# Last norm token-major with the store, weight splits moved to VectorE and ahead, and the router's transpositions placed among the rows'

## The reference, cut to what matters

```python
def _rmsnorm(x, g):
    return x * rsqrt(mean(x * x, axis=-1) + EPS) * g

# layer 0: Hyena channels, two orders, then the output projection
for o in range(HYENA_ORDER):
    z = gates[o] * _fftconv(z, kf[:, o], p['filt_bias'][o])
yl = concatenate([y_a, z]) @ p['w_out']

# layer 1: conformer
u = h @ p['cf_w1'] + p['cf_b1']
u = u[..., :D_MODEL] * sigmoid(u[..., D_MODEL:])
u = _dwconv_vertical(u, p['cf_dw_w'], p['cf_dw_b'], rows)
yl = silu(_layernorm(u, p['cf_ln_g'], p['cf_ln_b'])) @ p['cf_w2'] + p['cf_b2']

# both layers
xl = xl + g1 * yl
h = _modulate(_rmsnorm(xl, norm2_g[l]), sh2, sc2)
probs = softmax(einsum('bnd,de->ben', h, router), axis=experts)
gates, idx = top_k(probs, cap)          # every expert takes its 64 best tokens
xl = xl + g2 * (experts' outputs, weighted and added back)

return _rmsnorm(xl, final_g)
```

## Time and profile before

| | us |
|---|---|
| median of 3 runs | 3064.94 (3060.89 to 3071.62) |
| profiled execution, device time | 3064.76 |
| its span | 3063.0 |
| PE busy, of the span | 2473.9 (81%) |
| PEld | 1524.5 (50%) |
| DVE | 1330.0 (43%) |
| ACT | 601.3 (20%) |
| POOL | 266.8 (9%) |

### The profile page before, as it was taken

The page is one execution under the profiler, slowest core; times in us unless marked ns, Lnnn a source line. Parts: engine busy times, 40 slices in busy tenths (PEclk is TensorE's granted clock), DMA queues, the critical chain, the costliest instruction groups (busy, mean ns, idle before and its releaser), DMA issues. The chain is left out here.

```text
span 3063.0 us, 42592 instructions
## 1 busy us (share of the span) xinstructions
PE 2473.9 (81%) x18456; PEld 1524.5 (50%) x18456; DVE 1330.0 (43%) x2123; ACT 601.3 (20%) x868; POOL 266.8 (9%) x165
## 2 busy tenths in 40 slices
PE   5987499888999997359366678998986787889896
PEld 3775499764554553337223463443435564434343
DVE  4876755445232323469545641211216843112214
ACT  3333311122111111432400130110003132100011
POOL 2000000111000000120302230000003211000000
PEclk7997599988999998679658789999998888999998
DMA  4580111145999994157010329999983135999994
GB/s 150 179 281 12 35 39 39 45 166 247 418 407 418 417 418 169 55 170 243 22 47 28 112 83 416 427 428 428 428 340 83 55 139 220 427 428 428 428 427 193
DMA packets 123082, 726.90 MB, mean 237 GB/s; under 512 B 11958, under 2 KB 67510, under 8 KB 85879
## 3 DMA queue, kind: packets, MB, share of 16 engines
q1 hardware_dynamic: 92776, 695.79, 56.1%
q10 hardware_dynamic: 30160, 28.97, 2.9%
HBM read 722.63 MB, written 2.10 MB: 237 GB/s over the span
## 5 line engine op out<-in xcount | busy, mean ns | idle before, releaser
L1962 PE MATMUL ps<-s_ring,s_c_XG 128*64 128x512 f32 x1280 | 351.0, 615 | 57.5 <-DMA s_ring<-in_exp_w 25.7
L332 PE MATMUL ps<-s_h_part,s_w_hi 128*128 128x512 f32 x944 | 300.1, 400 | 77.2 <-PEq L433 62.9
L2074 DVE TENSOR_TENSOR s_c_hid<-ps,s_c_sil 128x512 f32<-128x512 f32 x32 | 34.3, 1073 | 515.2 <-PE ps L1962 515.2
L1962 PEld LDWEIGHTS ps<-s_ring,s_c_XG 128*64 128x64 f32 x1280 | 118.0, 141 | 279.2 <-issue 278.0
L1962 PE MATMUL ps<-s_ring_at,s_c_XG 128*64 128x512 f32 x768 | 238.1, 627 | 22.9 <-DMA s_ring_at<-in_exp_w 19.2
L332 PEld LDWEIGHTS ps<-s_h_part,s_w_hi 128*128 128x128 f32 x944 | 181.7, 194 | 121.9 <-issue 72.2
L2003 PE MATMUL ps<-s_ring_at,s_c_hidT 128*64 128x512 f32 x768 | 223.2, 593 | 0.0
L1962 PE MATMUL ps<-s_ring,s_m_XG 128*64 128x512 f32 x768 | 222.7, 593 | 0.0
L332 PE MATMUL ps<-s_h_part,s_w_lo 128*128 128x512 f32 x472 | 187.4, 397 | 0.0
L373 DVE CUSTOM_DVE_ANT_0 s_mod_w<-s_mod_w,s_mod_silu 128x1024 f32<-128x1024 f32 x112 | 135.1, 1221 | 42.8 <-DMA s_mod_w<-in_vectors 42.6
L1962 PEld LDWEIGHTS ps<-s_ring,s_m_XG 128*64 128x64 f32 x768 | 71.1, 137 | 142.7 <-issue 141.6
(11 more groups left out here) (584 smaller groups left out, 4434.0 us busy)
## 6 DMA issues: line engine op xcount, KB each, us to landing
s_ring<-in_exp_w SPq DMA_DIRECT2D x96, 2048.0 KB, 16.4
s_ring_at<-in_exp_w SPq DMA_DIRECT2D x96, 2048.0 KB, 18.6
s_ring<-in_moe_w_gate SPq DMA_DIRECT2D x32, 2048.0 KB, 12.2
s_ring_at<-in_moe_w_down SPq DMA_DIRECT2D x32, 2048.0 KB, 12.3
s_mod_w<-in_vectors SPq DMA_DIRECT2D x112, 512.0 KB, 4.5
s_ring<-in_moe_w_up SPq DMA_DIRECT2D x16, 2048.0 KB, 12.7
s_ring_at<-in_moe_w_up SPq DMA_DIRECT2D x16, 2048.0 KB, 16.3
s_w_raw<-in_w_in ACTq DMA_DIRECT2D x21, 1024.0 KB, 7.7
```

The source lines that it names most:

```text
L332: last = nc.tensor.matmul(bank, w[a][:, i % 2, k, c0:c0 + P], x[b][:, k, at], start=start, stop=stop)
L1962: last = nc.tensor.matmul(ps[x * SLOTS:(x + 1) * SLOTS, bank + fh, :], XG[:, k, c0:c0 + SLOTS], w[x][:, at:at + 512], start=(k == 0), stop ...
L2074: nc.vector.tensor_tensor(hid_out[:, fh * per:(fh + 1) * per, :], ps[:, UP + fh, :].rearrange("s (p j) -> s p j", j=nj), sil[:, fh * 512:( ...
```

## The change

1. The last norm and the store become one block, `norm_and_store`. TensorE transposes `xT` itself; per token tile ScalarE squares both halves from PSUM and sums them along the row in the same instruction, VectorE makes the mean of squares, ScalarE the root, VectorE the reciprocal of one column and two multiplies from PSUM by it and by the gains. The gains are tiled over the partitions on the host (`final_g_2_row`, 512 KB) and loaded by SyncE behind the last refill of the last expert pass, into a fixed place.
2. In `conformer_in` the lower halves of units 2 to 7 are made by VectorE, between `u` of m and its taps. GpSimd has nothing there.
3. In `residual_route_choice` the transpositions of `wts` stand behind the fifth of the eight row groups and write to the `LOGITS` bank; the last row group, which needs that bank, waits for VectorE's copy. The subtraction of one is done by the last copy out of PSUM.
4. In `hyena_conv`, order 1, ScalarE and VectorE split units 0 and 1 of `w_out_2`, once `B` is written.

```diff
@@ tensor_tiles ends with the sums; its last loop becomes
-                for j, (n, half) in enumerate(self.rows):
+            def tensor_rows(self, pe, first, end):
+                for j in range(first, end):
+                    n, half = self.rows[j]
                     if self.ROW_BANKS[j] == self.SUMS:
                         pe.wait_ge(self.ms_done.sem, 1)
                     if self.ROW_BANKS[j] == self.LOGITS:
@@ residual_route_first
                     R.tensor_tiles(pe, 1)
+                    R.tensor_rows(pe, 0, 2 * KT)
@@ residual_route_choice
-            PROBS, RANK = R.ROW_BANKS[0], R.ROW_BANKS[1]
+            PROBS, RANK = R.LOGITS, R.ROW_BANKS[1]
...
                     R.tensor_tiles(pe, P)
-                    pe.wait_ge(R.row_out.sem, 2)
+                    R.tensor_rows(pe, 0, 5)
                     pe.wait_ge(dve_out.sem, v0 + 2)
                     for t in range(KT):
                         last = nc.tensor.transpose(ps[0:E, PROBS, t * P:(t + 1) * P], wts[:, t, :], ident)
                     last.then_inc(*mm_done.up())
+                    R.tensor_rows(pe, 5, 2 * KT - 1)
                     pe.wait_ge(dve_out.sem, v0 + 3)
+                    R.tensor_rows(pe, 2 * KT - 1, 2 * KT)
+                    pe.wait_ge(R.row_out.sem, 2)
+                    pe.wait_ge(dve_out.sem, v0 + 4)
...
-                    vlink(V.tensor_copy(work[0][:], ps[0:E, PROBS, :]))
+                    V.tensor_copy(work[0][:], ps[0:E, PROBS, :]).then_inc(*dve_out.up())
+                    dve.wait_ge(dve_out.sem, dve_out.n)
...
-                    vlink(V.tensor_tensor(rk[:], rk[:], sel[:], ALU.mult))
-                    V.tensor_scalar(rk[:], rk[:], -1.0, None, ALU.add).then_inc(*dve_out.up())
+                    V.tensor_tensor(rk[:], rk[:], sel[:], ALU.mult).then_inc(*dve_out.up())
                     dve.wait_ge(mm_done.sem, m0 + 2)
-                    V.tensor_copy(rankm[:], ps[:, RANK, 0:KT * E].rearrange("p (t e) -> p t e", t=KT))
+                    V.tensor_scalar(rankm[:], ps[:, RANK, 0:KT * E].rearrange("p (t e) -> p t e", t=KT), -1.0, None, ALU.add)
@@ experts_pass, end of SyncE's list
+                        if load_also is not None:
+                            load_also(sp)
@@ hyena_conv, ScalarE and VectorE
+                        if o == HYENA_ORDER - 1:
+                            act.wait_ge(dve_out.sem, v0 + HF)
+                            ahead.split_hi(act, 0)
+                            ahead.split_hi(act, 1)
+                            ahead.early = True
...
+                        if o == HYENA_ORDER - 1:
+                            ahead.split_lo_unit(dve, 0)
+                            ahead.split_lo_unit(dve, 1)
                         for c in range(CT):
                             dve.wait_ge(mm_done.sem, m0 + 2 * HF + c + 1)
@@ conformer_in
-                    @block.gpsimd
-                    def _(pool):
-                        W.split_lo(pool, W.next_unit())
...
+                        for i in range(W.next_unit(), 2):
+                            W.split_lo_unit(dve, i)
                         for m in range(KD):
                             dve.wait_ge(act_out.sem, a0 + m + 1)
                             nc.vector.scalar_tensor_tensor(u[:, m, :], ps[:, 2 * (m % 4), :], vcol("cf_b1_2", m), sig[:, m % 2, :], ALU.add, ALU.mult).then_inc(*dve_out.up())
+                            W.split_lo_unit(dve, m + 2)
@@ store_result becomes norm_and_store(gain, gain_here)
                         for t in range(KT):
-                            sp.wait_ge(dve_out.sem, v0 + t + 1)
-                            sp.wait_ge(act_out.sem, a0 + t + 1)
+                            sp.wait_ge(scaled_rows.sem, 2 * t + 2)
                             sp.dma_start(out[t * P:(t + 1) * P, :], rows[:, t, :]).then_inc(*stored.up(16))
...
-                                    last = nc.tensor.transpose(ps[:, 2 * t + half, c * P:(c + 1) * P], src[:, half * 4 + c, t * P:(t + 1) * P], ident)
-                                last.then_inc(*mm_done.up())
+                                    last = nc.tensor.transpose(ps[:, 2 * t + half, c * P:(c + 1) * P], xT[:, half * 4 + c, t * P:(t + 1) * P], ident)
+                                last.then_inc(turned.sem, 1)
...
                         for t in range(KT):
-                            act.wait_ge(mm_done.sem, m0 + 2 * t + 2)
-                            nc.scalar.activation(rows[:, t, 512:1024], ps[:, 2 * t + 1, :], ACT.Copy).then_inc(*act_out.up())
+                            for half in range(2):
+                                act.wait_ge(turned.sem, 2 * t + half + 1)
+                                nc.scalar.activation(square[:, half, :], ps[:, 2 * t + half, :], ACT.Square, accum_out=part[:, t, half:half + 1]).then_inc(summed.sem, 1)
+                            act.wait_ge(meaned.sem, t + 1)
+                            nc.scalar.activation(root[:, t:t + 1], ms[:, t:t + 1], ACT.Sqrt).then_inc(rooted.sem, 1)
...
+                        dve.wait_ge(gain_here.sem, 16)
                         for t in range(KT):
-                            dve.wait_ge(mm_done.sem, m0 + 2 * t + 1)
-                            nc.vector.tensor_copy(rows[:, t, 0:512], ps[:, 2 * t, :]).then_inc(*dve_out.up())
+                            at = slice(t, t + 1)
+                            dve.wait_ge(summed.sem, 2 * t + 2)
+                            vlink(V.tensor_tensor(ms[:, at], part[:, t, 0:1], part[:, t, 1:2], ALU.add))
+                            V.tensor_scalar(ms[:, at], ms[:, at], 1.0 / D, RMS_EPS, ALU.mult, ALU.add).then_inc(meaned.sem, 1)
+                            dve.wait_ge(rooted.sem, t + 1)
+                            vlink(V.reciprocal(rstd[:, at], root[:, at]))
+                            for half in range(2):
+                                to = slice(half * 512, (half + 1) * 512)
+                                V.scalar_tensor_tensor(rows[:, t, to], ps[:, 2 * t + half, :], rstd[:, at], gain[:, to], ALU.mult, ALU.mult).then_inc(scaled_rows.sem, 1)
@@ calls
+        def load_final_gain(sp):
+            at = vec_at["final_g_2_row"]
+            sp.dma_start(final_gain[:], A["vectors"][:, at:at + D]).then_inc(final_gain_here.sem, 16)
...
-            moe_choice(1, W, hT, weight(1, 1), part(1, 3), part(1, 5), part(1, 2), vcol("cf_b2_2", 0, KD))
-        with ExitStack() as last:
-            fin = sbuf(last, "fin", [P, KD, T])
-            rms_norm(xT, fin, T, lambda k: vcol("final_g_2", k))
-            store_result(fin)
+            moe_choice(1, W, hT, weight(1, 1), part(1, 3), part(1, 5), part(1, 2), vcol("cf_b2_2", 0, KD), load_final_gain)
+        norm_and_store(final_gain, final_gain_here)
```

21 lines of the change are left out of this document (16 added, 5 removed).

## The result

The changed kernel takes **3032.39 us** (median of 4 runs, 3030.24 to 3033.6), the kernel before 3063.02 in the same comparison (4 runs, 3060.89 to 3071.62). The ratio is 0.9903 with a 95% interval of 0.9889 to 0.9917: 30.6 us faster, by the interval 25 to 34. The forecast was 3036, its range 3028 to 3046.

A forecast was written before the change was run, and what follows sets the result against it. DMA engines were taken to bound both expert passes of the second model, so gains came from chains ahead and outside. 8.2 + 3.5 + 4.5 + 13.0 = 29.2 us off 3064.76 gave 3035.6, stated as 3036, range 3028 to 3046.

The forecast's parts named there:

- first rival: Expert passes: DMA-bound, they might end when they did, so router-stage gains vanish; costs 3.5 + 4.5, 3044 us; chance 8%.
- Conformer, 8.2: Conformer: VectorE making six lower halves itself ends its last unit at 2428.9 instead of 2437.1, saving 8.2 us.
- second rival: Conformer: 1.0 us wait paid each time, or splits and taps over 10.88; saves 2 or less, 3042 us; chance 14%.
- Hyena, 3.5: Router stage behind the order-1 Hyena block: with two units split early, first product 1.50 us in instead of 4.98, saving 3.5.
- band of 2.5 us either way: TensorE's restart behind the Hyena block: 3.5 us earlier, it may keep the higher clock or meet the low one longer.
- taken up while TensorE makes the next 128 channels: Hyena block: the early splits just fit VectorE's idle time behind B; a few tenths over cost nothing.
- fifth rival: Hyena block: memory for the early split not free or units no earlier; that gain is 0, 3039 us; chance 6%.
- Routers, 4.5: Two routers: weights' transpositions ahead of 12 for the rows, subtraction of one off the chain; 2.25 us each, 4.5 both.
- transposition's 1.8: Each router: 20 instead of 32 row transpositions stand ahead of the weights'; 12 x 0.167 = 2.0, taken as 1.8 us.
- The -1: Each router: subtracting one leaves the chain and rides on the last copy from PSUM, saving 0.45 us with its link.
- Tail, 13.0: Last norm and store: first tile done at 3039.7, three more at 2.27 us, then 3.45 to the end; 13.0 us less.
- third rival: Last norm: Square and Sqrt switch tables, seven further loads of 1.28, 9.0 us, giving 3045 us; chance 2%.

The follow-up runs named there:

- second profile: The changed kernel run and profiled once more with nothing altered, as the mark for three further kernels: median 3032.83 us.
- the part alone: The kernel before with only the last norm and store changed: median 3051.41 us, ratio 0.9946 to 0.9974.

## Why the prediction was right, and where not

**The bound.** It was right to look at the head of each pass and not at its length. From the router's last copy of layer 0 to the end of the conformer's table load, with the DMA-bound pass between, it is 511.9 us before, 510.1 in the changed kernel and 511.9 in its second profile, so what is won ahead of this pass is kept, and in one of two profiles 1.8 us more.

In layer 1 it is not all kept. From the last copy of the router to VectorE's last addition, it is 479.7 us before, 480.9 and 481.4 in the changed kernel's two profiles, 481.1 to 481.3 in the six other kernels with the new order, and 479.2 to 480.4 in the six with the old one, of which the kernel before is one and the kernel with the order alone undone, 479.8, another. So 1.2 to 1.7 of the 1.9 us that the second router wins are given back behind it, about as much as the order wins, and the first rival holds for that term. Windows of 4 us, 3.8 us behind that last copy, before and in the changed kernel:

```profile
2558.00:2562.00 4.00, 4.00 (x29) 4.00 (x29) 0.24 (x1) 0.84 (x2) 0.00 (x0) 0.79 0.00 0
```

```profile
2536.50:2540.50 4.00, 4.00 (x26) 4.00 (x25) 0.00 (x0) 0.84 (x2) 0.00 (x0) 0.66 0.00 0
```

The granted clock is 0.79 before and 0.66 after: the chain is done sooner, the end of the low clock behind it is not, and the first refill is issued 18.9 us behind the last copy where it was 18.4. That is 0.5 us of the loss. From first refill to last the two passes take 424.0 and 425.7 us before, 425.5 and 423.9 in the changed kernel, so neither moved by the 2 us that the forecast named as a sign of being wrong; but from layer 1's last refill to VectorE's last addition it is 38.2 where it was 35.7. Why the end of the pass does not follow its refills is open.

**Conformer, 8.2.** Measured 8.2, in every profile that has it, and by the mechanism forecast. The wait of 1.05 us in the first unit leaves VectorE 0.9 us behind. From then on its units start every 10.88 us, TensorE's own pace, and hold a wait of 0.17 or 0.18 us for the upper half each, so that VectorE's own work is 10.7 us a unit, a little less than the 10.8 of the forecast. The second rival's conditions were not met: splits and taps stay under 10.88, and what is paid each time is 0.18 us and not 1.0. The two units without a split take the lag away.

**Hyena, 3.5.** Measured 3.4, or 6.5 where the clock stays up. The prediction had the second case as a band of 2.5 us either way; it is a second level 3.1 us below, in four of nine profiles, and none fell on the other side. Not all of the 3.1 lasts: from the Hyena sums to the end of layer 0's pass the changed kernel takes 575.5 us in its first profile and 574.4 in its second, against 582.5 before. The step "taken up while TensorE makes the next 128 channels" held: VectorE's last addition in the block starts 17.7 us behind the block's sums before and after. So the fifth rival, units that come no earlier, is out.

**Routers, 4.5.** Measured 3.9 in the routers themselves, 1.5 and 0.4 each (3.6 in the second profile), and less by the end of layer 1's pass, as told above. The term mis-sized is the transposition's 1.8. In layer 0 the four transpositions do start 2.0 us sooner behind the weights' last write, 0.32 us after it in the place of the 2.33 of the kernel with the order undone; but that moves them into a window of lower clock, and they take 1.06 us instead of 0.60:

```profile
1792.00:1794.00 2.00, 2.00 (x12) 1.85 (x11) 0.94 (x5) 1.96 (x4) 0.00 (x0) 0.50 0.99 426
```

In layer 1 they take 0.60, and start 0.80 us after the write in the place of 2.33, behind the first 20 for the rows, 3.83 us or 0.19 each. The 12 that now come later are cheaper:

```profile
2516.46 1.59 PE L1512 MATMUL ps<-s_base,s_hT_l 128*128 128x128 f32 x12
```

That is 0.13 each, where the forecast took the mean of all 32, 0.167. And in layer 0 the low clock falls on the one or the other: in the second profile the four take 0.60 there, but the 20 ahead of them take 3.97 and not 3.40, and the copy waits 1.57 us. The -1 measured 0.39, not 0.45.

**Tail, 13.0.** Measured 14.1, in the part alone 13.4. Three terms were off. The eight transpositions were costed at 0.199 each, from a row at the lower clock; in the changed kernel 32 take 3.68, 0.115 each, and the block starts at a granted clock of 1.00. In the part alone it is 0.50 there, and 32 take 5.30:

```profile
3038.00:3040.00 2.00, 2.00 (x11) 2.00 (x10) 0.32 (x2) 1.81 (x5) 0.00 (x0) 0.50 0.00 0
```

A tile takes 2.13 instead of 2.27, since the two small instructions take 0.33 with the link between them, not 0.4, and the next tile's first one begins 0.08 before the multiplies end. And from the last multiply to the end of the span it is 3.05 us, not 3.45. The forecast's own terms up to tile 0 add up to 3039.5, and not to the 3039.7 that it goes on with. The read of the accumulator, the forecast's upper bound of 0.4 a tile, is there, and hidden from the second tile on, as ScalarE waits 0.77 for the mean.

**Tables.** One load, as predicted. The third rival's 9.0 us were seven more loads in full; with six more, 7.7 us, the tail took 5.9 more, since they also fill the 0.77 us that ScalarE waited in each of three tiles.

**The sum.** 8.2 + 3.4 + 3.9 + 14.1 = 29.6 where 29.2 was forecast; the medians say 30.6 and 30.3. In the first profile layer 0's pass adds 1.8, the norm behind the conformer up to the next router 1.0, layer 1's pass takes 1.2 back and the blocks ahead of the conformer 0.1: 31.1 us from the Hyena sums to the end. In the second the four are 6.5 + 8.2 + 3.6 + 14.1 = 32.4, the same three stretches -0.1, +1.1 and -1.7: 31.7. So it is in part luck that the sum came out so close: the tail's term was 1.1 too small, the routers' 0.6 too large and in part given back, the Hyena term has two levels, and the stretches between add what no term had. The forecast's 3036 lies 3.6 above the median, and 1.9 of that is its starting point: it starts from 3064.94, the median of three runs, and the kernel before has 3063.02 in the comparison. The other 1.7 lie within what the medians resolve.

## What to carry to other kernels

Long GpSimd instructions are not free hands beside a busy VectorE: in this kernel a 4.8 us split costs VectorE about 4.1, and a pair of equal products takes 1.67 us where VectorE alone needs 1.20 for both. Count such work on GpSimd as work on VectorE, unless VectorE is idle then, or its instruction is like the u of these rows, with one of its inputs in PSUM. Read a gain in the stretch around its edit and not in the span, then once more at the end of the stage behind it, where some of it may be given back. And when an experiment's end number comes out as expected, look at the instructions as well: a loss just under another engine's pace leaves the same number.

## What the runs showed of the hardware

- A VectorE instruction with one input can be held as those with two are, and by a GpSimd copy as by a subtraction: a VectorE instruction of 0.54 us took 4.07 beside a GpSimd split, and GpSimd's one-input copies of 1.90 and 1.97 held two of VectorE's for 0.84 and 1.50 us.
- After the same pause of 2.11 us at the same place TensorE's granted clock fell to 0.50 in one execution of the changed kernel and stayed at 1.00 in another; with pauses of up to 1.7 us, four in 96 us, it was 0.99 over these 96.
- A chain that is done 1.9 us sooner ahead of layer 1's pass did not bring the end of the low clock forward by as much: 0.66 granted in the window behind it where it was 0.79, and the pass 1.2 to 1.7 us longer.
- A square with a running sum is two ScalarE instructions, 0.60 and 0.20 us. Square needed no table load after silu nor after the root.
- Two executions differ by 10 us in one unedited stretch of 287, and with it the granted clock there (0.64 or 0.81 in a window of 50 us).
